# A hybrid decoder trunk: attention's opening moved ahead of the last value unit, and a second output unit moved into the early steps

## The chip, the cores and the metric

The kernel runs on one core of a Trainium2 chip. The metric is the device time of one execution in microseconds (us). A core has a matrix engine (TensorE, PE in the profile), a vector engine (VectorE, DVE), an activation engine (ScalarE, ACT), GpSimd (POOL) and SyncE (SP), which here issues the DMAs. Each engine works through its own list of instructions in order, and the lists are tied together by semaphores that the kernel sets and waits for by hand.

## The reference

Two layers over 512 tokens of width 1024. Each layer normalizes x, projects it once, and feeds the parts of the projection to four mixers (differential attention, a short gated convolution, an S5 state-space mixer with a gated output, a Mamba-2 mixer). Their outputs, 1280 channels together, go through one output projection; a gated MLP follows. The part around the change is this:

```python
for l in range(DEPTH):
    proj = rmsnorm(x, ln1_g[l]) @ w_in[l]
    ...
    # per head h of 4, per block i of 128 queries, for c in (0, 1):
    s = q[c] @ k[c].T                      # causal, scaled, q and k normalized and rotated
    p[c] = softmax(s)
    o = (p[0] - lam * p[1]) @ v            # then rmsnorm over the head's 128 channels
    ...
    g = gelu(y); o_c = g * sigmoid(g @ w_glu + b_glu)     # the S5 mixer's gate
    x = x + concat(o_a, o_b, o_c, o_d) @ w_out[l]
```

## The kernel before

**Weights come as units.** Each projection is cut into units of 128 output channels. For unit g, SP loads the weights into a raw buffer, ACT copies them to a high part `wh` (`prep`, line 1105), POOL subtracts to get the low part `wl` (`low`, line 430), and PE multiplies three times: high weights by the low and by the high part of the input, low weights by the high part. `wh` and `wl` have two buffers, used in turn. PE's `unit` (line 582) does an output or MLP unit into a bank of PSUM; `v_unit` (line 898) does one of four units of the value projection, which gather over all four into banks 0, 1, 6 and 7. These four are input units 24 to 27, the last of the input stage.

**Attention** is 16 steps, n = 0 to 15: head n // 4, query block n % 4. A step's width is 128, 256, 384 or 512 keys. Its parts are handed round the engines:

- PE `scores(n)`: the two score matrices, into banks 2 and 3 for even n, 6 and 7 for odd n.
- DVE `maxima(n)`: two row maxima. ACT `exps(n)`: two exponentials with their sums. DVE `combine(n)`: reciprocals, scaling and the difference of the two, into G.
- PE `turn(n)`: transposes that into bank 4. ACT copies it back to G (line 1363). PE `attend(n)`: multiplies by v into bank 5, one bank for each head.
- When a head is complete: DVE `head_out` copies bank 5 to `ssum`, ACT `head_square` squares it, PE `head_sum` sums it over the channels into the bank that `HEAD_BANK = [0, 0, 2, 6]` gives, ACT `head_log` and `head_rms` and DVE `head_emit` normalize.

PE runs `scores(0)` and `scores(1)` after the fourth value unit, and then in step n: `scores(n + 2)`, `turn(n)`, `attend(n - 1)`. The head sum of head 0 stands at the end of step 6, that of head 1 at the end of step 10.

**Beside the steps** PE does other work. Eight output units over the channels of mixers B and D ("early" units) can be done before attention is complete; six of them stand in the steps that `BESIDE = [1, 5, 7, 9, 13, 15]` names, between `turn` and `attend` (that of step 15 ahead of its turn), the two others behind step 15. They go into banks 0 and 1 in turn, by their place in the list. DVE's `residual` (line 1504) adds a finished one to x and frees the bank; it stands at the head of the following step. The S5 gate (`s5_glu`, two banks, 0 and 1) stands in step `GATES = 3`; ACT then loads the sigmoid's table, computes two sigmoids and loads the table of exp and ln again, DVE multiplies, and in the next step ACT and DVE split the result (`emit`, `emit_low`).

**Order on DVE.** In step n DVE does `combine(n + 1)` and `maxima(n + 2)`; the maxima come first in the steps that `MAXIMA_AHEAD = (1, 3, 4, 10, 11)` names. **Order on ACT.** In step n: `exps(n + 1)`, the copy of turn n, then the gate's part, `head_square`, a `prep` in the step after a unit, `head_log`.

**Banks are claimed.** PE waits before it writes a bank until what it held was read; `claim` notes who frees it:

```python
def claim(b, freed, k=1):
    if b in free_at:
        pe.wait_ge(*free_at[b])
    free_at[b] = (freed, raised(freed, k))
```

`unit` claims its bank with `resid` (DVE's residual frees it), and `head_sum(b)` claims bank b with `head_ln`, after it has waited for the square.

Of the kernel before, what the change touches and what calls it, by code (L numbers as in the profile page):

```python
# [11 lines left out]
ACT = mybir.ActivationFunctionType  # L12
# [3 lines left out]
D, T, P = 1024, 512, 128  # L16
KD = D // P
NQ = T // P
# [9 lines left out]
KLATE, KEARLY = MIXB, MIXED - MIXB  # L28
STEPS = HEADS * NQ
# [5 lines left out]
PAIR_STEPS, PAIR_HIGHS, PAIR_LOWS, PAIR_SUBS, PAIR_SUMS, PAIR_READS = 13, 6, 3, 4, 4, 6  # L35
PAIR_BANKS = [(6, 7, 4, 5), (2, 3, 0, 1)]
GROUPS = -(-2 * SJ // BLOCKS)
BESIDE = [1, 5, 7, 9, 13, STEPS - 1]
GATES = 3
MAXIMA_AHEAD = (1, 3, 4, 10, 11)  # L40
V_BANK = [0, 1, 6, 7]
HEAD_BANK = [0, 0, 2, 6]
WHOLE_MEAN = 5
# [36 lines left out]
def build(nc, A):  # L80
    with ExitStack() as ctx:
# [485 lines left out]
        def _(pe):  # L567
# [6 lines left out]
# [4 lines that stand above are left out]
                if freed is xbc_silu:  # L578
                    raised(unit_out)
                free_at[b] = (freed, raised(freed, k))  # L580
# [344 lines left out]
                    w = mm(bank[4][:, t:t + 1], rbc[:, t * P:(t + 1) * P], ident[:, 0:1], start=True, stop=True)  # L925
                w.then_inc(act_bank[4], 1)

            def scores(n):
                h, q = n // NQ, n % NQ
                banks = (2, 3, 6, 7)[2 * (n % 2):2 * (n % 2) + 2]  # L930
                rows = [slice(QK * c, QK * c + QK) for c in range(2)]
                qs = [qk[r, 2 * h, q * P:(q + 1) * P] for r in rows]
                last = slice(q * P, (q + 1) * P)
                for b in banks:
                    claim(b, exp_done)
                if q:
                    for c, b in enumerate(banks):
                        mm(bank[b][:, 0:q * P], qs[c], qk[rows[c], 2 * h + 1, 0:q * P], start=True, stop=True)  # L938
                for c, b in enumerate(banks):
                    mm(bank[b][:, last], qs[c], qk[rows[c], 2 * h + 1, last], start=True, stop=False)  # L940
                for b in banks:
                    mm(bank[b][:, last], cbf[:, 0, :], cbf[:, 1, :], start=False, stop=True).then_inc(dve_bank[b], 1)
# [31 lines left out]
            for l in range(L):  # L974
# [22 lines left out]
                        s5_windows(l, 0)  # L997

                for s in range(2, NIN):
                    if s >= NIN - NQ:  # L1000
                        v_unit(l, s - (NIN - NQ))
                    else:
                        unit(unit_bank(s), KD, xh, xl, xbc_silu if 2 <= s <= 7 else unit_out,
                             within=lambda: beside(s - 1))
                    if s == 2:
                        dt_turn()
                    if s == 8:
                        s5_inputs(l, 3)
                    if s == 7:
                        pe.wait_ge(xbc_silu, 6 * l + 4)  # L1010
                        m2_turn(0)
                        m2_turn(1)
                    if s == 9:
                        m2_turn(2)
                        m2_turn(3)
                        pe.wait_ge(xbc_silu, 6 * l + 6)
                        m2_states(0)
                        m2_states(1)
                    if s == 10:
                        m2_states(2)  # L1020
                        s5_kernels(l)
                    if s == 11:
                        m2_decays(1)
                        s5_windows(l, 1)
                        s5_in(l, 0)
                    if s == 12:
                        m2_apply(0)
                        m2_decays(2)
                        m2_scores(1)
                    if s == 13:  # L1030
                        m2_decays(3)
                    if s == 15:
                        m2_apply(1)
                    if s == 16:
                        m2_norm()
                    if 17 <= s <= 24:
                        qk_mean(l, s - 17)
                    if s == 25:
                        token_norm()
                    if s == 22:  # L1040
                        s5_out(l, 1)
                beside(NIN - 1)

                pe.wait_ge(qk_done, 8 * (l + 1))
                pe.wait_ge(mask_ready, 1)
                scores(0)
                scores(1)
                for n in range(STEPS):
                    if n + 2 < STEPS:
                        scores(n + 2)  # L1050
                    if n == BESIDE[-1]:
                        unit(1, KEARLY, early_hi, early_lo, resid)
                    turn(n)
                    if n == GATES:
                        s5_glu()
                    if n == BESIDE[0]:
                        pe.wait_ge(mixed_ready, nth(mixed_ready, KEARLY))
                    if n in BESIDE[:-1]:
                        unit(BESIDE.index(n) % 2, KEARLY, early_hi, early_lo, resid)
                    if n == 1:  # L1060
                        pe.wait_ge(v_ready, HEADS * (l + 1))
                    if n:
                        attend(l, n - 1)
                    if n > NQ and n % NQ == 2:
                        head_sum(HEAD_BANK[n // NQ - 1])
# [18 lines left out]
        def _(act):  # L1084
# [127 lines left out]
            for l in range(L):  # L1212
# [47 lines left out]
                def v_copy(t):  # L1260
# [3 lines left out]
                        act.wait_ge(act_bank[V_BANK[t]], nth(act_bank[V_BANK[t]]))  # L1264
                    fn(v[:, t, :], bank[V_BANK[t]][:, :], ACT.Copy, scale=token_rms[:, t:t + 1]).then_inc(v_ready, 1)

                for s in range(1, NIN):
                    prep()
                    if 6 <= s <= 10:
# [55 lines left out]
                    if s == 26:  # L1325
                        gelu(0)
                        gelu(1)
                        ln_exp_tables()

                def exps(n):  # L1330
                    w, s = (n % NQ + 1) * P, n % 2
                    for c in range(2):
                        act.wait_ge(exp_go, nth(exp_go))
                        fn(G[:, 2 * s + c, 0:w], bank[(2, 3, 6, 7)[2 * s + c]][:, 0:w], ACT.Exp,  # L1334
                           bias=soft[:, s, c:c + 1], accum_out=soft[:, s, 2 + c:3 + c]).then_inc(exp_done, 1)

                def head_square():
                    act.wait_ge(head_copied, nth(head_copied))
# [11 lines left out]
                act.wait_ge(token_ready, l + 1)  # L1350
                v_copy(2)
                v_copy(3)
                exps(0)
                v_copy(0)
                v_copy(1)
                for n in range(STEPS):
# [84 lines left out]
        def _(dve):  # L1441
# [554 lines left out]
            for l in range(L):  # L1996
# [4 lines left out]
                for s in range(2, NIN):  # L2001
# [86 lines left out]
                    if s in (21, 25):  # L2088
                        s5_finish(l, (s - 21) // 4)
                maxima(0)  # L2090
                maxima(1)
                combine(l, 0)
                for n in range(STEPS):
                    if n - 1 in BESIDE:
                        residual(BESIDE.index(n - 1), BESIDE.index(n - 1) % 2)
                    if n in MAXIMA_AHEAD:
                        maxima(n + 2)
# [1 line left out]
                        combine(l, n + 1)  # L2099
                    if n + 2 < STEPS and n not in MAXIMA_AHEAD:  # L2100
                        maxima(n + 2)
                    if n == GATES:
                        for i, (gate, gated) in enumerate(((sA, sC), (sB, sD))):
                            dve.wait_ge(glu_full, nth(glu_full))
                            tt(gated[:, :].rearrange("p (c t) -> p t c", t=CH),
                               *[k.rearrange("p (t c) -> p t c", t=CH) for k in (gate[:, :], u[:, i, :])],
                               MUL).then_inc(em_full, 1)
# [167 lines left out]
```

## Time and profile before

| what | value |
|---|---|
| median of 3 runs | 1295.24 us |
| range of the runs | 1295.24 to 1295.95 us |
| the profiled execution | 1294.14 us |
| its span, first to last instruction | 1292.4 us |
| PE busy | 1282.8 us (99%) |
| DVE busy | 996.9 us (77%) |
| POOL busy | 636.7 us (49%) |
| ACT busy | 533.6 us (41%) |

The profile is of one execution. Its time is 1.7 us longer than its span, and 1.1 us shorter than the median of the runs. The timeline view, of which most rows below are, lists instructions by start; neighbours of one kind are merged into a row with their count. The ends of PE's matmuls are modelled and overlap the start of the next, so the distance from start to start is what an instruction takes of PE's time. Attention lies at about 206 to 258 us in layer 0 and at about 844 to 896 us in layer 1.

### The profile page before, as it was taken

The numbers are of one execution on the slowest core, as the hardware profiler recorded it, in microseconds if no ns is written. First come the engines' busy times: TensorE is split into PE (matmuls) and PEld (weight loads), VectorE is DVE, ScalarE is ACT, GpSimd is POOL, SyncE is SP. The second block draws the span as 40 slices with busy tenths as digits, with TensorE's granted clock in tenths as the row PEclk, the third lists the DMA queues.
The fourth block names the chain that finished last, engine by engine and source line by source line (L and its number), as shares of the span: only waits on it lengthen the run. The fifth ranks groups of instructions, "written<-read, shape, count | busy, mean of one in ns | idle before, by whom it ended". The sixth has DMA issues, their size and how long they took to land.

```text
span 1292.4 us, 17677 instructions
## 1 busy us (share of the span) xinstructions
PE 1282.8 (99%) x6790; PEld 1075.5 (83%) x6790; DVE 996.9 (77%) x1376; ACT 533.6 (41%) x836; POOL 636.7 (49%) x314
## 2 busy tenths in 40 slices
PE   9999999999999999999999999999999999999999
PEld 6888887788888998888878888877888889888898
DVE  8789895846899868876237798777478998689997
ACT  6332556644333422233334235476442333323342
POOL 2986661244445344444458775612444443444532
PEclk9999999999999999999999999999999999999999
DMA  6232321033333233333233213211333333232323
GB/s 225 82 99 66 91 88 42 26 97 114 98 86 128 91 91 96 98 98 112 84 99 98 82 54 112 80 30 53 99 102 95 97 101 120 91 96 87 125 96 103
DMA packets 40947, 120.59 MB, mean 93 GB/s; under 512 B 6432, under 2 KB 10656, under 8 KB 40864
## 3 DMA queue, kind: packets, MB, share of 16 engines
q1 hardware_dynamic: 40864, 119.46, 29.8%
q8 instruction: 54, 0.88, 0.3%
q14 instruction: 29, 0.24, 0.1%
HBM read 114.20 MB, written 2.10 MB: 90 GB/s over the span
## 4 chain that ended last, share of the span: by engine, by line
PE 91%; DVE 4%; POOL 2%; ACT 2%; DMA 1%; issue 0%; SPq 0%; POOLq 0%
PE bank L599 22%; PE bank L612 22%; PE bank L604 21%; PE bank L650 12%; PE bank L911 3%; PE bank L959 1%; POOL wl L430 1%; DMA raw<-in_w_in 1%; PE bank L601 1%; PE bank L938 1%; PE bank L948 1%; PE bank L856 1%; ACT G L1334 1%; PE bank L789 1%; PE bank L804 1%; PE bank L813 1%
## 5 line engine op out<-in xcount | busy, mean ns | idle before, releaser
L430 POOL TENSOR_TENSOR wl<-raw,wh 128x1024 fp32r<-128x1024 f32 (+3 forms) x184 | 441.5, 2401 | 512.9 <-ACT wh L1105 423.5
L599 PE MATMUL bank<-xl,wh 128*128 128x512 f32 x1088 | 279.8, 395 | 0.7 <-DVE xl L1461 0.7
L612 PE MATMUL bank<-xh,wl 128*128 128x512 f32 x1088 | 272.4, 392 | 0.0
L604 PE MATMUL bank<-xh,wh 128*128 128x512 f32 x1056 | 261.0, 389 | 0.0
L1105 ACT ACTIVATE wh<-raw 128x1024 fp32r<-128x1024 f32 (+3 forms) x184 | 185.8, 1010 | 144.7 <-PE bank L604 81.2
L599 PEld LDWEIGHTS bank<-xl,wh 128*128 128x128 f32 x1088 | 202.4, 188 | 48.2 <-issue 4.3
L612 PEld LDWEIGHTS bank<-xh,wl 128*128 128x128 f32 x1088 | 203.2, 188 | 43.0 <-issue 1.4
L604 PEld LDWEIGHTS bank<-xh,wh 128*128 128x128 f32 x1056 | 198.2, 188 | 41.6
L447 POOL TENSOR_TENSOR wl<-raw,wh 128x768 fp32r<-128x768 f32 (+1 forms) x36 | 65.2, 1813 | 99.4 <-ACT wh L1109 67.8
L1406 ACT ACTIVATE G<-G 128x512 f32<-128x512 f32 x44 | 27.8, 633 | 181.4 <-DVE G L1487 181.4
L1109 ACT ACTIVATE wh<-raw 128x640 fp32r<-128x640 f32 (+2 forms) x72 | 60.4, 862 | 91.9 <-DVE raw L1922 32.7
L1504 DVE TENSOR_TENSOR x<-x,bank 128x512 f32<-128x512 f32 x40 | 27.4, 685 | 80.2 <-PE bank L612 80.0
L1475 DVE TENSOR_TENSOR G<-bank,rbc 128x512 f32<-128x512 f32 x68 | 46.5, 684 | 34.1 <-PE bank L612 34.1
L1475 DVE TENSOR_TENSOR pad<-bank,rbc 128x512 f32<-128x512 f32 x60 | 41.2, 687 | 39.5 <-PE bank L612 28.6
L599 PE MATMUL bank<-ml,wh 128*128 128x512 f32 x248 | 68.9, 401 | 0.0
L1487 DVE SCALAR_TENSOR_TENSOR G<-pad,par_all,G 128x512 f32<-128x512 f32 x48 | 66.5, 1385 | 1.7
L1482 DVE TENSOR_SCALAR G<-pad,par_all 128x512 f32<-128x512 f32 x48 | 65.5, 1365 | 1.6
L612 PE MATMUL bank<-mh,wl 128*128 128x512 f32 x248 | 63.3, 389 | 0.0
L1907 DVE TENSOR_TENSOR x<-x,bank 128x256 f32<-128x256 f32 (+1 forms) x72 | 41.7, 593 | 21.5 <-PE bank L667 16.3
L604 PE MATMUL bank<-mh,wh 128*128 128x512 f32 x225 | 57.2, 390 | 0.0
L1889 DVE TENSOR_TENSOR wl<-raw,wh 128x640 fp32r<-128x640 f32 x48 | 53.3, 1130 | 4.4 <-ACT wh L1109 4.3
L1167 ACT ACTIVATE xh<-x,par_all 128x512 fp32r<-128x512 f32 x32 | 23.1, 721 | 79.6 <-DVE x L1504 77.6
(345 smaller groups left out, 2097.2 us busy)
## 6 DMA issues: line engine op xcount, KB each, us to landing
raw<-in_w_gu SPq DMA_DIRECT2D x88, 512.0 KB, 3.6
raw<-in_w_in SPq DMA_DIRECT2D x52, 512.0 KB, 3.8
raw<-in_w_dn SPq DMA_DIRECT2D x32, 704.0 KB, 4.1
raw<-in_w_ol SPq DMA_DIRECT2D x16, 384.0 KB, 3.1
raw<-in_w_oe SPq DMA_DIRECT2D x16, 256.0 KB, 2.6
x<-in_x SPq DMA_DIRECT2D x8, 256.0 KB, 5.8
raw<-in_w_first SPq DMA_DIRECT2D x4, 512.0 KB, 4.1
out_x<-x SPq DMA_DIRECT2D x8, 256.0 KB, 4.8
```

What stands on the lines that cost most here:

```text
L430: tt(wl[:, p, 0:cols], raws[RAW[g][0]][:, 0:cols], wh[:, p, 0:cols].bitcast(F32), ALU.subtract).then_inc(wl_full, 1)
L447: tt(wl[:, p, cols], raws[PAIR_RAW[load][0]][:, cols], wh[:, p, cols].bitcast(F32), ALU.subtract).then_inc(pair_low, 1)
L599: mm(bank[b][:, :], wh[:, p, k * P:(k + 1) * P], lo[:, k, :], start=(k == 0), stop=False)
L604: w = mm(bank[b][:, :], wh[:, p, k * P:(k + 1) * P], hi[:, k, :], start=False, stop=False)
L612: w = mm(bank[b][:, :], wl[:, p, k * P:(k + 1) * P], hi[:, k, :], start=False, stop=(k == K - 1))
L650: i = mm(out, w[:, at[0], at[1] + k * P:at[1] + (k + 1) * P], b, start=start and k == 0, stop=stop and k == KW - 1, skip_group_check=True)
L1105: fn(wh[:, p, 0:cols], raws[r][:, 0:cols], ACT.Copy).then_inc(wh_full, 1)
L1109: fn(wh[:, p, to], raws[PAIR_RAW[2 * j + p][0]][:, of], ACT.Copy).then_inc(pair_high, 1)
L1475: tt(out, bank[b][:, :].rearrange(order, **sizes), rbc[:, :].rearrange(order, **sizes), MUL).then_inc(unit_out, 1)
L1482: after(ts(out, pad[:, p, 4:4 + T], weights[n - 1], None, MUL))
L1487: return stt(out, pad[:, p, 5 - n:5 - n + T], weights[0], out, MUL, ADD)
L1889: tt(wl[:, p, to], of, wh[:, p, to].bitcast(F32), SUB).then_inc(pair_sub, 1)
```

## The change

`scores(0)`, `maxima(0)`, `exps(0)` and `combine(0)` move ahead. PE does `scores(0)` before the fourth value unit, ACT does `exps(0)` before the `prep` of the loop's last step, and DVE does `combine(0)` before `maxima(1)`. After the last value unit PE does `scores(2)` and then `scores(1)`. The unit of step 7 moves to step 2, and the units of steps 1 and 2 (`UNIT_AHEAD`) stand ahead of the step's scores instead of behind its turn. The gate moves from step 3 to step 4. On DVE the maxima come first in other steps, and in steps 2, 3, 6 and 14 (`ADD_LATE`) the residual stands behind `combine` and `maxima`. The wait before a score bank is written is now spelled out by the step's number, since the steps' scores are no longer issued in order. `HEAD_BANK` and `unit` are as before.

```diff
-BESIDE = [1, 5, 7, 9, 13, STEPS - 1]
-GATES = 3
-MAXIMA_AHEAD = (1, 3, 4, 10, 11)
+BESIDE = [1, 2, 5, 9, 13, STEPS - 1]
+GATES = 4
+MAXIMA_AHEAD = (0, 1, 5, 6, 7, 11)
+UNIT_AHEAD = (1, 2)
+ADD_LATE = (2, 3, 6, 14)
...
-            def scores(n):
+            def scores(l, n):
...
-                for b in banks:
-                    claim(b, exp_done)
+                for c, b in enumerate(banks):
+                    if b in free_at:
+                        pe.wait_ge(*free_at[b])
+                    free_at[b] = (exp_done, 2 * (STEPS * l + n) + c + 1)
...
                 for s in range(2, NIN):
+                    if s == NIN - 1:
+                        pe.wait_ge(qk_done, 8 * (l + 1))
+                        pe.wait_ge(mask_ready, 1)
+                        scores(l, 0)
                     if s >= NIN - NQ:
                         v_unit(l, s - (NIN - NQ))
...
-                pe.wait_ge(qk_done, 8 * (l + 1))
-                pe.wait_ge(mask_ready, 1)
-                scores(0)
-                scores(1)
+                def early_unit(n):
+                    if n == BESIDE[0]:
+                        pe.wait_ge(mixed_ready, nth(mixed_ready, KEARLY))
+                    unit(BESIDE.index(n) % 2, KEARLY, early_hi, early_lo, resid)
+
+                scores(l, 2)
+                scores(l, 1)
                 for n in range(STEPS):
-                    if n + 2 < STEPS:
-                        scores(n + 2)
+                    if n in UNIT_AHEAD:
+                        early_unit(n)
+                    if 0 < n < STEPS - 2:
+                        scores(l, n + 2)
                     if n == BESIDE[-1]:
-                        unit(1, KEARLY, early_hi, early_lo, resid)
+                        early_unit(n)
                     turn(n)
                     if n == GATES:
                         s5_glu()
-                    if n == BESIDE[0]:
-                        pe.wait_ge(mixed_ready, nth(mixed_ready, KEARLY))
-                    if n in BESIDE[:-1]:
-                        unit(BESIDE.index(n) % 2, KEARLY, early_hi, early_lo, resid)
+                    if n in BESIDE[:-1] and n not in UNIT_AHEAD:
+                        early_unit(n)
...
                         gelu(0)
                         gelu(1)
                         ln_exp_tables()
+                        exps(0)
...
                 v_copy(2)
                 v_copy(3)
-                exps(0)
                 v_copy(0)
                 v_copy(1)
...
                 maxima(0)
+                combine(l, 0)
                 maxima(1)
-                combine(l, 0)
                 for n in range(STEPS):
-                    if n - 1 in BESIDE:
+                    if n - 1 in BESIDE and n not in ADD_LATE:
                         residual(BESIDE.index(n - 1), BESIDE.index(n - 1) % 2)
                     if n in MAXIMA_AHEAD:
                         maxima(n + 2)
...
                     if n + 2 < STEPS and n not in MAXIMA_AHEAD:
                         maxima(n + 2)
+                    if n - 1 in BESIDE and n in ADD_LATE:
+                        residual(BESIDE.index(n - 1), BESIDE.index(n - 1) % 2)
```

## Rows read from the trace of the kernel before

**Rows 1.** The page: busy us of each engine, share of the span, instructions.

```profile
PE 1282.8 (99%) x6790; PEld 1075.5 (83%) x6790; DVE 996.9 (77%) x1376; ACT 533.6 (41%) x836; POOL 636.7 (49%) x314
```

**Rows 2.** The waits of PE: total us, times, longest.

```profile
PE bank L938 <- ACT G L1334: 2.7, 6, 0.5
```

**Rows 3.** Timeline of PE, opening of attention in layer 0: start, duration, line.

```profile
202.02 1.98 PE L911 MATMUL bank<-wh,xh 128*128 128x512 f32 x8
203.84 1.98 PE L911 MATMUL bank<-wl,xh 128*128 128x512 f32 x8
205.74 0.49 PE L940 MATMUL bank<-qk 64*128 64x128 f32 x4
...
207.03 0.28 PE L942 MATMUL bank<-cbf 128*128 128x128 bf16 x2
207.71 0.70 PE L938 MATMUL bank<-qk 64*128 64x256 f32 x4 [0.40 <-ACT G L1334]
...
208.57 0.28 PE L942 MATMUL bank<-cbf 128*128 128x128 bf16 x2
...
209.78 0.92 PE L938 MATMUL bank<-qk 64*128 64x384 f32 x4 [0.50 <-ACT G L1334]
```

**Rows 4.** Timeline of ACT and DVE in the same stretch.

```profile
204.09 0.63 ACT L1105 ACTIVATE wh<-raw 128x512 fp32r<-128x512 f32 x1 [1.04 <-PE bank L911]
204.63 1.25 ACT L1265 ACTIVATE v<-bank,token_rms 128x512 f32<-128x512 f32 x2
...
206.43 0.49 DVE L1833 TENSOR_REDUCE soft<-bank 128x1 f32<-128x128 f32 x2 [9.34 <-PE bank L942]
```

**Rows 5.** Timeline of PE, steps 4 to 10 of layer 0.

```profile
221.93 0.29 PE L942 MATMUL bank<-cbf 128*128 128x128 bf16 x2
222.05 0.28 PE L948 MATMUL bank<-cst,G 128*128 128x128 f32 x1
222.17 1.06 PE L959 MATMUL bank<-G,v 128*128 128x128 f32 x8
223.68 0.92 PE L938 MATMUL bank<-qk 64*128 64x384 f32 x4 [0.45 <-ACT G L1334]
...
231.11 0.28 PE L942 MATMUL bank<-cbf 128*128 128x128 bf16 x2
231.46 0.66 PE L948 MATMUL bank<-cst,G 128*128 128x128 f32 x4
...
236.56 1.06 PE L959 MATMUL bank<-G,v 128*128 128x128 f32 x8
...
243.34 1.02 PE L967 MATMUL bank<-pad,cst 128*128 128x512 f32 x2
```

**Rows 6.** Timeline, all engines, from the gate's end to step 7.

```profile
220.31 0.83 PE L959 MATMUL bank<-G,v 128*128 128x128 f32 x6
...
220.51 0.69 ACT L1367 ACTIVATE s5b<-bank,par_all 128x512 f32<-128x512 f32 x1 [0.73 <-PE bank L813]
...
222.51 0.47 ACT L1334 ACTIVATE G<-bank,soft 128x256 f32<-128x256 f32 x1
...
223.58 0.64 ACT L1195 ACTIVATE mh<-s5c 128x512 fp32r<-128x512 f32 x1
...
224.62 0.59 ACT L1334 ACTIVATE G<-bank,soft 128x384 f32<-128x384 f32 x1
...
225.74 0.40 ACT L1363 ACTIVATE G<-bank 128x256 f32<-128x256 f32 x1
...
228.38 0.69 ACT L1334 ACTIVATE G<-bank,soft 128x512 f32<-128x512 f32 x1 [1.21 <-DVE soft L1833]
...
228.86 0.68 DVE L1504 TENSOR_TENSOR x<-x,bank 128x512 f32<-128x512 f32 x1
...
229.86 0.17 DVE L1840 RECIPROCAL soft<-soft 128x2 f32<-128x2 f32 x1 [0.32 <-ACT G L1334]
...
231.31 0.48 DVE L1833 TENSOR_REDUCE soft<-bank 128x1 f32<-128x128 f32 x2
```

More of the change, by code:

```diff
@@ L1265, in v_copy, with exps @@
                     fn(v[:, t, :], bank[V_BANK[t]][:, :], ACT.Copy, scale=token_rms[:, t:t + 1]).then_inc(v_ready, 1)
+                def exps(n):
+                    w, s = (n % NQ + 1) * P, n % 2
+                    for c in range(2):
+                        act.wait_ge(exp_go, nth(exp_go))
+                        fn(G[:, 2 * s + c, 0:w], bank[(2, 3, 6, 7)[2 * s + c]][:, 0:w], ACT.Exp,
+                           bias=soft[:, s, c:c + 1], accum_out=soft[:, s, 2 + c:3 + c]).then_inc(exp_done, 1)
                 for s in range(1, NIN):
@@ L1328, in _ @@
                         ln_exp_tables()
[L1330 to L1335, printed above, removed]
+                        exps(0)
                 def head_square():
```

## The prediction, made before the changed kernel was run

> **What bounds the kernel now.** I read the page first. PE is busy for 1282.8 us, 99% of the span [rows 1], so PE's list sets the end, and no PE instruction is added or removed. The change can give only what PE waits for inside attention, and can cost only new waits there. Second, the waits of PE: it waited 6 times for the exponentials before it could write a score bank [rows 2], which is three times in each layer. This view's 2.7 us is low, since modelled ends cover part of each wait. So I went, third, to PE's timeline and measured from start to start.
>
> Two prices come from a place without a wait. The two mask matmuls (L942) take 222.05 − 221.93 = 0.12 us, and a turn of one block takes 222.17 − 222.05 = 0.12 us [rows 5]. An `attend` of four blocks is eight such matmuls of 128 columns, 8 × 0.122 = 0.98 us, so the scores of step 5 could have begun at 222.17 + 0.98 = 223.15.
>
> Against these prices PE loses, in layer 0:
>
> - before `scores(2)`: 207.71 − 207.03 − 0.12 = 0.56 us [rows 3];
> - around `turn(0)` and before `scores(3)`: 209.78 − 208.57 − 2 × 0.12 = 0.97 us [rows 3] (`turn(0)` waits for `combine(0)`, then the scores for `exps(1)`);
> - before `scores(7)`: 223.68 − 223.15 = 0.53 us [rows 5]. `exps(5)` stands behind the sigmoids and two table loads;
> - before `turn(7)`: 231.46 − 231.11 − 0.12 = 0.23 us [rows 5].
>
> Together 2.29 us. Layer 1 shows the same waits, so 4.58 us is the most that these four can give. That is 0.35% of the time. About 0.2%, or 2.6 us, is what a measurement of this kernel can tell from no change.
>
> **The change part by part.**
>
> *The opening, −1.53 us a layer.* `scores(0)` now stands before the fourth value unit, whose three passes of 203.84 − 202.02 = 1.82 us [rows 3] run from 200.2 to 205.65. DVE has been idle for 9.34 us when `maxima(0)` comes at 206.43 [rows 4], so it takes the maxima at once, near 201.4. ACT is idle for 1.04 us before 204.09 [rows 4]. `exps(0)` starts in that hole, at 203.05, and takes less than 223.58 − 222.51 = 1.07 us, which holds a wider pair and a copy [rows 6]; so it delays nothing by more than 0.03. `combine(0)` follows on an idle DVE and takes less than the widest one's 1.45 (below): done before 205.6. `turn(0)` needs it only after 207, so that wait goes. `scores(2)` finds its banks free, so the 0.56 goes. The value unit runs 0.6 to 0.7 us later and pulls `prep` and the value copies with it: the two that `scores(1)` needs end near 205.88 + 0.7 = 206.6 [rows 4], and `scores(1)` comes near 207.4 because `scores(2)` is ahead of it. That is hidden by 0.8 us. `scores(3)` needs `exps(1)`: `scores(1)` ends near 208.2, its maxima take half a microsecond, and the exponentials at most the 1.07, so near 209.8; ahead of it PE now has the unit of step 1 (2.8 us), so it comes near 211.2. The 0.97 goes as well. Of the unit of step 2 the same holds: behind it stand `scores(4)`, `turn(2)` and `attend(1)`, whose inputs come some 0.5 us or more before they are needed. Without the unit as cover, `scores(4)` would wait as `scores(3)` did, up to 0.97 us.
>
> *Splitting the value units, +0.15 us a layer.* PE goes over from value to score matmuls twice instead of once. Before, that step costs 205.74 − (203.84 + 1.82) = 0.08 us [rows 3]. The way back is shown nowhere. I take 0.15 in all: below, nothing, if the weight loads overlap; above, 0.32, four such steps.
>
> *The gate a step later, −0.53 us a layer.* `exps(5)` now stands before the sigmoids, so `scores(7)` finds it done. `scores(8)` needs `exps(6)`, which ends about 3.4 us after the gate's matmuls (0.20 + 2.00 + 1.12, below). PE gets there only after about 5.4 us, with the unit of step 5 between. The gate's second bank was last used by the unit of step 2. Its residual ends near 220.7 and the matmuls for that bank begin near 222.0, so it is hidden by 1.3 us.
>
> *DVE's new order, −0.23 us a layer.* `combine(7)` is done before PE comes to `turn(7)`, because of the next term.
>
> *A new wait at the head sum, +2.07 us a layer.* The unit of step 5 was second in the list of units and used bank 1. Now it is third and uses bank 0. The head sum of head 0 stands in step 6 and claims bank 0. So PE cannot begin it before `residual` has freed the bank, and in step 6 this residual is one of those put behind `combine(7)`, which needs `exps(7)`. I count from the end of the gate's last matmul, E (220.31 in rows 6).
>
> ACT and DVE: the second sigmoid starts at E + 0.20. It and a table load take 222.51 − 220.51 = 2.00. `exps(6)` is 384 wide: 225.74 − 224.62 = 1.12. The copy of turn 5 is 256 wide: 0.40, of which 0.10 overlaps, so 0.30. Two `emit` and the `head_square` take 0.52 each, by (224.62 − 223.58) / 2: together 1.56. `exps(7)` to the reciprocal is 229.86 − 228.38 = 1.48. `combine(7)` is 231.31 − 229.86 = 1.45. The residual is 0.68, and 0.06 more until PE sees it [all rows 6]. The sum is 0.20 + 2.00 + 1.12 + 0.30 + 1.56 + 1.48 + 1.45 + 0.68 + 0.06 = 8.85 us.
>
> PE in the same time: `attend(3)`, `scores(7)`, `turn(5)`, the unit, `attend(4)`, `scores(8)`, `turn(6)`, `attend(5)`. Steps 7 to 10 of before hold the same pieces in the same widths and order, from `attend(7)` to the head sum of head 1, without a wait: 243.34 − 236.56 = 6.78 us [rows 5].
>
> PE is at the head sum 8.85 − 6.78 = 2.07 us too early. Bounds: 1.7 if ACT's instructions overlap by 0.04 us more each; 2.5 if DVE is last instead. DVE's own list (gate products, `head_out`, `maxima(7)`, `combine(6)`, two `emit_low`, `maxima(8)`) comes out only 0.1 us ahead of ACT. Queued behind the waiting head sum is all of PE. ACT's `head_log` waits for the sum, and `exps(8)` stands behind it. Step 7 has no unit any more. By the same prices `scores(10)` and `turn(8)` still find their inputs some 0.2 us early.
>
> The Trainium skill speaks against this sum at one place. "ScalarE: Activation LUTs", section "What ACT_TABLE_LOAD costs", gives every change of table about 1.38 us of drain beside its load of 1.28 us. Rows 6 show 2.00 us for sigmoid (0.69) and load together, so there is no room for a drain and I use the row. By the page the stall would be 1.38 us longer.
>
> *Prep, POOL and the DMAs.* The third and fourth weights of this stage are prepared in steps 2 and 3 instead of 2 and 6, each ahead of its use by several us. SP's and POOL's lists keep their order; I price this at nothing, since the unit that uses the fourth comes only in step 9. If ACT's extra 0.5 us in step 3 were not covered, `exps(5)` would be that much later, and it has 4 us.
>
> Sum for a layer: −1.53 + 0.15 − 0.53 − 0.23 + 2.07 = −0.07 us. For two layers it is −0.14 us, on the profiled execution's 1294.14 us; the median of the runs is 1.1 us above that, so I forecast 1295.24 − 0.14 = 1295.1 us.
>
> **The rivals.**
>
> *The head sum does not wait.* If bank 0 is free in time (the residual early, or ACT's chain 2 us shorter than I make it), the gain stays: 2 × (−2.14) = −4.3 us, 1291.0 us. For it speaks that my chain has nine terms. Against it: every one is read from a row, and all nine would have to be half a term wrong in one direction.
>
> *The opening gives half.* If `turn(0)` or `scores(3)` still waits (value copies late behind `prep`), 0.75 us a layer is lost: 1296.6 us. The margins of 0.5 to 0.8 us speak against it.
>
> *Steps 8 to 10 come apart (slower).* After the late head sum, `head_log`, `exps(8)`, `head_rms` and the copy of turn 7 run one behind the other on ACT with no unit on PE as cover. If they are over 0.2 us slower than I make them, `scores(10)`, `turn(8)` and `scores(11)` wait as the narrow steps of the opening did. The price is that of the waits of before at the same kinds of place, 0.56 + 0.97 + 0.53 = 2.06 us a layer: 1295.1 + 4.1 = 1299.2 us. It decides from the 0.2 us on. Against it: these parts are short and read from rows of the same widths.
>
> *A drain at the tables (slower).* If something follows the second table load that rows 6 do not show, the head sum waits longer by it. It would take 1.3 us a layer to matter: 1295.1 + 2.6 = 1297.7 us. The page's 1.38 us would make it 1297.9 us. Rows 6 speak against it.
>
> **How the numbers follow.** The forecast has 0.70, the half opening 0.08, the head sum without a wait 0.12, steps 8 to 10 apart 0.08, the drain 0.02. The forecast's own range: the terms' bounds give a layer −2.29 + 0 + 1.7 = −0.59 to −2.29 + 0.32 + 2.5 = +0.53 us, so −1.2 to +1.1 us about 1295.24; the runs differ by 0.7 us, mostly upward: 1293.6 to 1297.0 us. To hold 8 in 10 it must reach into the others on both sides, to 1292.5 and 1297.5 us. Faster by over 0.2% (below 1292.6): the first rival and a tail of the forecast, 0.14. Slower by over 0.2% (above 1297.8): the last two, 0.10. Within: 0.76.
>
> **What the profile of after would show.** Right: in each layer no PE wait before `scores(2)`, `turn(0)`, `scores(3)` and `scores(7)`; `scores(0)` before the last three passes of L911; a gap of about 2 us before the first head sum (L967), which ends on DVE's residual (L1504); that residual behind the 512-wide `combine(7)`. Attention then begins earlier and ends where it ended. Wrong: a first head sum without a gap makes it 1291; gaps at L938 and L948 in steps 8 to 11 make it slower.

## The result, and the profile after

The changed kernel takes 1297.04 us, the kernel before 1295.15 us (medians of 21 runs each, in turn on the same chip). The ratio is 1.0015, with a 95% interval of 1.0009 to 1.0021. The forecast was 1295.1 us, so the change costs 1.9 us where I had it at nothing. 1297.04 lies inside the stated range of 1292.5 to 1297.5, and just outside the 1293.6 to 1297.0 that the forecast's own terms gave. Times, medians and ratios here leave out one disturbed run, one of the twelve of e7_gate3, which took 1419.12 us at a mean clock of 0.849.

The waits of PE in the changed kernel (total, times, longest) hold the forecast's new wait, and the six waits of [rows 2] are gone:

```profile
PE bank L971 <- DVE x L1515: 3.9, 2, 2.0
```

L971 is the head sum's matmul and L1515 the residual (L967 and L1504 before). Next, the timeline of PE: the opening and the steps to 7 in layer 0.

```profile
199.34 1.97 PE L913 MATMUL bank<-wl,xh 128*128 128x512 f32 x8
201.24 0.49 PE L944 MATMUL bank<-qk 64*128 64x128 f32 x4
...
205.50 1.98 PE L913 MATMUL bank<-wl,xh 128*128 128x512 f32 x8
207.41 0.70 PE L942 MATMUL bank<-qk 64*128 64x256 f32 x4
...
209.25 0.28 PE L952 MATMUL bank<-cst,G 128*128 128x128 f32 x1
209.29 1.17 PE L601 MATMUL bank<-ml,wh 128*128 128x512 f32 x4
...
212.20 0.92 PE L942 MATMUL bank<-qk 64*128 64x384 f32 x4
...
224.61 1.05 PE L963 MATMUL bank<-G,v 128*128 128x128 f32 x8
225.59 0.92 PE L942 MATMUL bank<-qk 64*128 64x384 f32 x4
...
230.96 0.61 PE L963 MATMUL bank<-G,v 128*128 128x128 f32 x4
233.52 1.30 PE L971 MATMUL bank<-pad,cst 128*128 128x512 f32 x2 [1.95 <-DVE x L1515]
234.75 0.80 PE L942 MATMUL bank<-qk 64*128 64x128 f32 x4
...
236.09 1.06 PE L952 MATMUL bank<-cst,G 128*128 128x128 f32 x4
236.95 1.19 PE L963 MATMUL bank<-G,v 128*128 128x128 f32 x6
238.07 0.70 PE L942 MATMUL bank<-qk 64*128 64x256 f32 x4
```

`scores(0)` stands at 201.24 inside the value units. After them, `scores(2)`, `turn(0)` (209.25), `scores(3)` (212.20) and `scores(7)` (225.59) follow on what is ahead of them without a wait, where [rows 3] and [rows 5] have gaps. PE comes to the head sum at 230.96 + 0.45 = 231.41 (an `attend` of four matmuls and 0.45 us, as at 229.06 and 229.51 before) and starts it at 233.52. The timeline of DVE shows what it waits for, the end of `combine(7)` and behind it the residual:

```profile
232.02 0.75 DVE L1853 SCALAR_TENSOR_TENSOR G<-G,soft 128x512 f32<-128x512 f32 x1
232.69 0.68 DVE L1515 TENSOR_TENSOR x<-x,bank 128x512 f32<-128x512 f32 x1
```

The rows behind the head sum are the news: the same matmuls take nearly twice as long as before the wait. The turn of four blocks takes 236.95 − 236.09 = 0.86 us, in layer 1 (below) 0.44. The windows view of the changed kernel shows why (the columns after the stretch: PE, PEld, DVE, ACT and POOL busy, the granted clock, DMA share, GB/s):

```profile
225.00:231.00 6.00, 6.00 (x42) 4.76 (x42) 5.67 (x12) 5.97 (x14) 0.00 (x0) 1.00 0.00 0
233.50:238.00 4.50, 4.48 (x22) 3.27 (x22) 1.70 (x6) 2.71 (x8) 0.40 (x1) 0.62 0.20 62
873.40:876.40 3.00, 2.96 (x22) 2.03 (x22) 0.99 (x4) 1.83 (x7) 0.42 (x1) 1.00 0.32 90
```

After the wait TensorE's granted clock is at the lower of its two levels, 1.2 instead of 2.4 GHz, for most of 233.5 to 238. In this execution that happened in layer 0 only. In layer 1 the clock stayed, and the timeline of PE shows the same wait and then the usual durations:

```profile
873.44 1.10 PE L971 MATMUL bank<-pad,cst 128*128 128x512 f32 x2 [1.95 <-DVE x L1515]
874.46 0.49 PE L942 MATMUL bank<-qk 64*128 64x128 f32 x4
...
875.23 0.60 PE L952 MATMUL bank<-cst,G 128*128 128x128 f32 x4
875.67 0.83 PE L963 MATMUL bank<-G,v 128*128 128x128 f32 x6
876.44 0.70 PE L942 MATMUL bank<-qk 64*128 64x256 f32 x4
```

From the head sum to `scores(10)` it is 238.07 − 233.52 = 4.55 us in layer 0 and 876.44 − 873.44 = 3.00 us in layer 1. The difference, 1.55 us, is the price of one fall. The runs agree. 18 of the changed kernel's 21 runs have a mean clock below 1.000. Their spans are 1294.9 to 1295.8 us where it is 0.999 (12 runs) and 1296.1 to 1297.8 us at 0.997 and less (6 runs). The three at 1.000 have 1292.8, 1293.4 and 1293.8 us; the kernel before has a median span of 1293.4 to 1293.6 us in its runs beside the experiments. So without the falls the change gives nothing, as the sum said, and with them it costs 1.9 us. An estimate: if 0.999 stands for one fall and the lower clocks for two, as in p1 and p2 below, there are 24 falls in 21 runs, and 24 / 21 × 1.55 = 1.8 us.

### The profile page after: what moved, and what is told of

Same layout as the page of the kernel before. It is cut to its first block, busy times and chain, and to the rows that moved or that the text cites. A ratio compares the mean times of both kernels' runs of the same rounds, so it can differ in the third digit from the quotient of the medians.

```text
span 1295.2 us, 17677 instructions
## 1 busy us (share of the span) xinstructions
PE 1283.8 (99%) x6790; PEld 1075.1 (83%) x6790; DVE 996.5 (77%) x1376; ACT 533.9 (41%) x836; POOL 636.5 (49%) x314
## 4 chain that ended last, share of the span: by engine, by line
PE 92%; DVE 4%; POOL 2%; DMA 1%; ACT 1%; issue 0%; SPq 0%; POOLq 0%
PE bank L601 22%; PE bank L614 22%; PE bank L606 21%; PE bank L652 12%; PE bank L913 3%; PE bank L963 1%; PE bank L942 1%; POOL wl L432 1%; DMA raw<-in_w_in 1%; PE bank L603 1%; PE bank L952 1%; PE bank L858 1%; PE bank L944 1%; PE bank L971 1%; PE bank L791 1%; PE bank L806 1%
## 5 line engine op out<-in xcount | busy, mean ns | idle before, releaser
L1515 DVE TENSOR_TENSOR x<-x,bank 128x512 f32<-128x512 f32 x40 | 27.4, 684 | 79.8 <-PE bank L614 79.7
```

## The experiments

**The head sum's wait taken away (e1_bank1).** Head 0's sum goes to bank 1, which nobody uses in step 6.

```diff
-HEAD_BANK = [0, 0, 2, 6]
+HEAD_BANK = [1, 0, 2, 6]
```

> The changed kernel with the first head sum in bank 1 instead of bank 0, so that it does not wait for the residual of the unit of step 5. Theory 1 (the wait of 2.0 to 2.1 us at the head sum costs its own length in each layer, and in some executions TensorE's granted clock falls to 1.2 GHz behind it, which costs some 1.6 us more each time): no wait at the first head sum, mean clock 1.000 in every run, 1297.0 - 2 x 2.1 - 1.9 = 1290.9 us, 0.3% below before, and runs close together. Theory 2 (the clock and the spread of the runs have nothing to do with this wait): the wait goes but the clock stays at 0.999 and below in most runs: about 1292.8 us, still spread over 5 us.

Measured: 1290.95 us (1290.75 to 1291.36), ratio 0.9967 (0.9955 to 0.9980), all five runs with clock 1.000 and spans of 1289.0 to 1289.6 us. The timeline of PE at the head sum:

```profile
230.68 0.61 PE L963 MATMUL bank<-G,v 128*128 128x128 f32 x4
231.13 1.02 PE L971 MATMUL bank<-pad,cst 128*128 128x512 f32 x2
```

The sum starts 0.45 us after the start of `attend(5)`, as without a wait. This constant decides the change: with it, a gain of 4.3 us; without, a loss of 1.9 us.

**The residual of step 6 early again (e2_resid_first).**

```diff
-ADD_LATE = (2, 3, 6, 14)
+ADD_LATE = (2, 3, 14)
```

> The changed kernel with the residual of step 6 at the head of the step again; the head sum stays in bank 0. Theory 1: DVE does the residual as soon as the unit is done, about 0.7 us after it and before the head sum comes, so the wait is gone or under 0.3 us: 1290.9 to 1291.5 us, clock 1.000. combine(7) comes 0.6 us later, which turn(7) does not feel. Theory 2: about 1292.8 us with a clock below 1. If not the residual but something else holds bank 0, the wait stays and the time is 1297.

Measured: 1293.04 us (1292.33 to 1296.51), ratio 0.9985 (0.9976 to 0.9994), ten of eleven runs at clock 1.000. The wait at the head sum went, but one that I had ruled out came. The timeline of PE:

```profile
231.24 1.10 PE L971 MATMUL bank<-pad,cst 128*128 128x512 f32 x2
...
232.91 0.28 PE L946 MATMUL bank<-cbf 128*128 128x128 bf16 x2
233.87 0.66 PE L952 MATMUL bank<-cst,G 128*128 128x128 f32 x4 [0.67 <-DVE G L1853]
```

`turn(7)` starts 0.96 us after the mask matmuls instead of 0.12: it waits for `combine(7)`. The residual pushes that back by 0.43 us only (its last instruction starts at 232.18, in e1_bank1 at 231.75). The larger part is that this instruction takes 1.64 us here and 0.75 in e1_bank1. The timelines of DVE and POOL in e2_resid_first, and behind the dots those of e1_bank1:

```profile
232.18 1.64 DVE L1853 SCALAR_TENSOR_TENSOR G<-G,soft 128x512 f32<-128x512 f32 x1
231.97 1.30 POOL L432 TENSOR_TENSOR wl<-raw,wh 128x512 fp32r<-128x512 f32 x1 [10.26 <-ACT wh L1116]
...
231.75 0.75 DVE L1853 SCALAR_TENSOR_TENSOR G<-G,soft 128x512 f32<-128x512 f32 x1
231.97 1.67 POOL L432 TENSOR_TENSOR wl<-raw,wh 128x512 fp32r<-128x512 f32 x1 [10.26 <-ACT wh L1116]
```

Here it begins 0.21 us after POOL's `low` and is the slow one of the two; in e1_bank1 it begins 0.22 us before, and POOL's is. Layer 1 has the same 1.64 us. Without it `combine(7)` would have been done just in time for `turn(7)`. That POOL's instruction is the reason is read from rows, here and in the last section, and was not tested.

**TensorE kept busy through the wait (e3_fill, e8_fill4).** Matmuls into the free bank 1, with a result that is used nowhere, ahead of the head sum of step 6, nine of them in the first kernel (below) and four in the second.

```diff
                     if n > NQ and n % NQ == 2:
+                        if n == NQ + 2:
+                            pe.wait_ge(*free_at[1])
+                            for _ in range(9):
+                                mm(bank[1][:, :], wh[:, 1, 0:P], early_hi[:, 0, :], start=True, stop=True)
                         head_sum(HEAD_BANK[n // NQ - 1])
```

> The changed kernel with nine matmuls of 128x512 (9 x 0.23 = 2.05 us) into bank 1, which is free there, ahead of the first head sum: their result is used nowhere. The head sum still starts when the residual is done, but TensorE is not idle before it. Theory 1: clock 1.000 in every run, 1295.0 to 1295.3 us, as before. Theory 2 (what costs the extra 1.9 us is not the idle time): 1297.0 us as in the changed kernel, with clocks below 1.

> As the kernel with nine matmuls ahead of the first head sum, but with four (0.9 us), so that TensorE is idle for some 1.1 us there instead of 2.0 or none. Taken by spans, since the kernel with nine lay 2.5 us under its time and not 1.8. Theory 1 (idle time at the head sum lets the granted clock fall, the more often the longer it is): clock below 1.000 in fewer runs than the 18 of 21 of the changed kernel and in more than the 3 of 11 with nine matmuls; median span between 1294.3 and 1295.2 us. Theory 2 (the number of falls has nothing to do with idle time): as often as in the changed kernel, 1295.2 us.

Measured with nine: 1296.57 us (1295.39 to 1298.64), ratio 1.0011 (1.0002 to 1.0020). Its time lies further above its span than in the other kernels (2.0 us in the median and up to 2.75, elsewhere 1.8), so spans are the better measure: the median is 1294.3 us, against 1295.2 in the changed kernel and 1293.5 in the kernel before beside it. The clock is 1.000 in 8 of 11 runs. Theory 1 had said all, and the time of before; of the 0.8 us that are missing, some 0.4 remain in the runs at 1.000 (median span 1293.9 against 1293.5 us), and I did not trace them. With four: 1295.61 us, ratio 1.0005 (0.9996 to 1.0014), median span 1293.8 us, idle 1.0 us at each head sum, clock 1.000 in 9 of 11 runs. Both theories missed here: theory 1 wanted more falls than with nine matmuls and a span of 1294.3 us or more. The timeline of PE with nine matmuls, and the window around it:

```profile
231.07 2.31 PE L1079 MATMUL bank<-mh,wh 128*128 128x512 f32 x9
233.28 1.10 PE L971 MATMUL bank<-pad,cst 128*128 128x512 f32 x2
```

```profile
231.00:236.00 5.00, 5.00 (x33) 3.54 (x33) 2.84 (x8) 2.51 (x8) 1.68 (x1) 1.00 0.19 52
```

The head sum starts as late as in the changed kernel, so the wait is all there. Only the idle time is gone, and with it most of the falls (3 of 11 runs instead of 18 of 21). So it is the idle time that brings the fall, not the late start. Going from nine matmuls to four, from no idle time to 1.0 us, adds no falls that these runs can show (3 and 2 of 11). The remaining ones contradict theory 1 as I had put it, with 1.000 in every run; p4 below shows one place where they can come from.

**The same wait in the kernel before (e4_before_wait).** Head sum in bank 1, which the unit of step 5 uses there, and the residual of step 6 behind `combine` and `maxima`.

```diff
-HEAD_BANK = [0, 0, 2, 6]
+HEAD_BANK = [1, 0, 2, 6]
...
-                    if n - 1 in BESIDE:
+                    if n - 1 in BESIDE and n != 6:
...
+                    if n - 1 in BESIDE and n == 6:
+                        residual(BESIDE.index(n - 1), BESIDE.index(n - 1) % 2)
```

> The kernel before with the same wait built in and nothing else of the change: first head sum in bank 1, which the unit of step 5 uses there, and the residual of step 6 behind combine(7) and maxima(8). From the rows of before the head sum would start at 232.45 instead of 229.51, 2.9 us late, of which 0.2 us replaces the wait before turn(7). Theory 1: a wait of 2.9 us in each layer with a fall of the clock behind it in most runs: 1295.2 + 5.4 + 1.6 to 3.2 = 1302 to 1304 us, clock 0.996 to 0.999. Theory 2: 1300.6 us, clock 1.000.

Measured: 1304.63 us (1303.33 to 1305.93), ratio 1.0071 (1.0059 to 1.0084), all five runs at 0.996 or 0.997. The waits of PE, and windows behind the two head sums:

```profile
PE bank L967 <- DVE x L1504: 5.8, 2, 2.9
```

```profile
233.00:238.00 5.00, 4.63 (x20) 2.98 (x21) 1.66 (x6) 2.53 (x8) 0.35 (x1) 0.66 0.18 56
...
876.00:881.00 5.00, 5.00 (x19) 3.08 (x20) 1.59 (x6) 2.64 (x8) 0.00 (x0) 0.50 0.19 52
```

The wait is 2.9 us as worked out, and 4.0 us more is lost: the clock falls behind both. In layer 1 the fall lasts about twice as long as the others that the traces show (the granted clock is 0.50 from about 875.5 to 882.3 us, elsewhere for 3 to 4 us). So wait and fall need nothing of the change but the bank and the residual's place.

**One wait instead of two (e9_wait_l0).**

```diff
+HEAD_BANK = [1, 0, 2, 6]
...
+                        head_sum(0 if l == 0 and n == 6 else HEAD_BANK[n // NQ - 1])
```

(and the same bank for ACT's `head_log`)

> The changed kernel with the first head sum in bank 0 in layer 0 only and in bank 1 in layer 1: one wait of 2.0 us instead of two. Theory 1: 1290.95 + 2.1 = 1293.1 us where the clock holds, and up to 1.7 us more in the runs in which it falls, so a median of 1293.1 to 1294.8, clocks of 1.000 and 0.999 and never below 0.998. Theory 2: 1293.1 us.

Measured: 1294.59 us (1292.85 to 1297.68), ratio 0.9996 (0.9987 to 1.0005). By the mean clock of the execution: four runs at 1.000 with spans of 1291.1 to 1291.6, four at 0.998 with 1292.6 to 1293.5, three at 0.996 or 0.997 with 1295.0 to 1295.9 us. At clock 1.000 the three kernels with two, one and no wait have median spans of 1293.4, 1291.3 and 1289.1 us, so each wait costs 2.1 to 2.2 us by itself. The three low runs contradict my expectation of at most one fall of 1.7 us.

**Where the falls stand (p1 to p4).** Profiles again: twice the changed kernel, twice the kernel with one wait.

> The changed kernel unchanged, for a second profile. Its first one fell in clock in layer 0 only. Theory 1: waits of 2.0 us at both first head sums again, and any stretch with a granted clock below 1.00 begins within a few us of one of them; which layers fall differs from execution to execution. Theory 2: a fall stands somewhere else in the span.

> The changed kernel unchanged, for a third profile: theory 1 as in the second (each fall within a few us of a wait at a first head sum), theory 2 a fall elsewhere.

> The kernel with the wait in layer 0 only, again: 3 of its 11 runs had a clock of 0.996 to 0.997 and spans 4 us above the fastest, more than one fall of 1.7 us. Theory 1a: the fall behind the one wait can last about twice as long, in one piece. Theory 1b: a second fall stands somewhere else, without a wait of this kind ahead of it. With a clock of 0.998 or 1.000 in this profile it stays open.

> The kernel with the wait in layer 0 only, a third profile: theory 1a one longer fall behind the wait if the clock is 0.997 or less, theory 1b a second fall somewhere else.

Measured (one execution each, beside 1294.37 us for the kernel before): p1 1296.55 us, clock 0.999, with a fall in layer 0 only; p2 1297.88 us, 0.997, with falls in both layers; p3 1292.99 us, 1.000, with none; p4 1296.04 us, 0.997, with a fall behind its one wait and another elsewhere. Windows of p2 behind the head sums of the two layers:

```profile
233.00:239.00 6.00, 5.71 (x34) 4.36 (x35) 3.17 (x10) 3.42 (x11) 0.68 (x1) 0.72 0.18 46
872.00:877.00 5.00, 4.02 (x19) 2.32 (x20) 1.39 (x4) 1.94 (x7) 1.36 (x1) 0.66 0.20 54
```

The windows of p4, and its waits:

```profile
10.00:15.00 5.00, 4.60 (x9) 2.06 (x9) 4.68 (x6) 3.82 (x8) 2.11 (x1) 0.66 1.04 406
235.00:241.00 6.00, 5.96 (x36) 4.69 (x37) 3.03 (x9) 3.53 (x12) 0.41 (x1) 0.72 0.18 46
```

```profile
PE bank L601 <- ACT wh L1116: 2.2, 1, 2.2
PE bank L971 <- DVE x L1515: 2.0, 1, 2.0
```

The second fall of p4 stands at the kernel's start. There TensorE had waited 2.2 us for the first weights, and in that execution longer than in the others (1.2 us at most in the other profiles). So this low run has a second fall, as theory 1b says, but again behind a wait of about 2 us. Theory 1a is not excluded for the low runs of e9_wait_l0, which have no profile: layer 1 of e4_before_wait has one fall of twice the usual length. The start is the same in every kernel here and can explain falls where the head sum is filled or does not wait; for those runs it was not looked at.

**The opening alone (e5_open_only).** The changed kernel with the constants of before and no unit ahead.

```diff
-BESIDE = [1, 2, 5, 9, 13, STEPS - 1]
-GATES = 4
-MAXIMA_AHEAD = (0, 1, 5, 6, 7, 11)
-UNIT_AHEAD = (1, 2)
-ADD_LATE = (2, 3, 6, 14)
+BESIDE = [1, 5, 7, 9, 13, STEPS - 1]
+GATES = 3
+MAXIMA_AHEAD = (1, 3, 4, 10, 11)
+UNIT_AHEAD = ()
+ADD_LATE = ()
```

> The opening alone: scores, maxima, exponentials and combination of step 0 ahead of the last value unit, with the units, the gate and DVE's order as before. By rows of before the waits ahead of scores(2) and turn(0) go (0.82 us a layer), but scores(3) now comes right behind turn(0), at about 208.4, and needs exps(1), done at 209.8: it starts near 209.95, where it started at 209.78 before. So the opening without a unit as cover gives nothing: theory 1: 1295.2 + 2 x 0.17 = 1295.6 us, and up to 3 us more where the clock falls behind the new wait of 1.5 us. Theory 2 (the opening gives its own share whatever stands ahead of scores(3)): 1295.2 - 2 x 0.7 = 1293.8 us.

Measured: 1295.42 us (1294.87 to 1297.52), ratio 1.0004 (0.9995 to 1.0013). The timeline of PE:

```profile
208.88 0.28 PE L952 MATMUL bank<-cst,G 128*128 128x128 f32 x1
210.65 0.92 PE L942 MATMUL bank<-qk 64*128 64x384 f32 x4 [1.49 <-ACT G L1282]
```

The kernel before is at 1295.14 us beside it. All the time won at `scores(2)` and `turn(0)` is lost again ahead of `scores(3)`. The early step 0 is worth something only with a unit ahead of `scores(3)`.

**The fast variant without the opening (e6_no_open).** `scores(0)` and `exps(0)` where they were, `combine(0)` behind `maxima(1)`, the rest as in e1_bank1.

```diff
-                    if s == NIN - 1:
...
-                        scores(l, 0)
...
+                scores(l, 0)
+                scores(l, 1)
                 scores(l, 2)
-                scores(l, 1)
...
```

(and the same on ACT, with `exps(0)` between the value copies, and on DVE)

> The fast variant (first head sum in bank 1) without the opening: scores(0), scores(1) and scores(2) after the last value unit, exps(0) behind the value copies as before; units, gate and DVE's order as changed. The waits ahead of scores(2) and turn(0) come back, 0.82 us a layer, and the split of the value units goes, 0.15: theory 1: 1290.95 + 2 x 0.67 = 1292.3 us. Theory 2 (most of the opening's gain comes from the early step 0, not from the unit ahead of scores(3)): 1290.95 + 2 x 1.4 = 1293.8 us.

Measured: 1292.87 us (1291.96 to 1294.34), ratio 0.9982 (0.9973 to 0.9991); at clock 1.000 a median span of 1290.8 us against 1289.1. The opening is worth 1.7 us with a unit as cover, 0.85 a layer, or 1.9 us by the median times. The timeline of PE, the first pass of the fourth value unit and `scores(3)`:

```profile
200.60 1.98 PE L913 MATMUL bank<-wh,xl 128*128 128x512 f32 x8
...
212.36 0.92 PE L942 MATMUL bank<-qk 64*128 64x384 f32 x4
```

That is 11.76 us, and in the changed kernel, from where the third value unit is done, 212.20 − 201.15 = 11.05: 0.71 us less, in layer 1 0.72. The two waits make 0.82, so splitting the value units costs 0.1 us. The rest of what the runs show, 0.1 to 0.3 us a layer, I did not trace.

**The fast variant with the gate in step 3 (e7_gate3).**

```diff
-GATES = 4
+GATES = 3
```

> The fast variant (first head sum in bank 1) with the gate in step 3 as before. exps(5) stands behind the sigmoids and two table loads again; with the units of steps 1 and 2 ahead nothing else covers it, so scores(7) waits by rows of before 0.53 us, less what one unit fewer behind it leaves: theory 1: 1290.95 + 2 x 0.53 = 1292.0 us. Theory 2 (the later gate gives nothing of its own): 1291.0 us.

Measured: 1297.88 us (1296.99 to 1301.38), ratio 1.0022 (1.0013 to 1.0031), some 7 us above e1_bank1 where I had expected 1. The waits of PE:

```profile
PE bank L952 <- DVE G L1853: 2.1, 2, 1.1
PE bank L942 <- ACT G L1282: 1.9, 2, 1.0
PE bank L815 <- DVE x L1515: 1.4, 2, 0.7
```

The gate now waits for the late residual of the unit of step 2, whose bank it needs. That pushes back its sigmoids, `exps(5)` and `combine(6)`, and each of them keeps PE waiting. So the gate's move is no gain of 0.5 us beside the others: with this order on DVE it is what makes the units of steps 1 and 2 possible. Whether an early residual in step 3 would do as well was not run.

**A last wait in the fast variant (e10_tuned).**

```diff
-MAXIMA_AHEAD = (0, 1, 5, 6, 7, 11)
-ADD_LATE = (2, 3, 6, 14)
+MAXIMA_AHEAD = (0, 1, 5, 6, 7, 9, 11)
+ADD_LATE = (2, 3, 6, 10, 14)
```

> The fast variant (first head sum in bank 1) with maxima(11) ahead of combine(10) in step 9 and the residual of step 10 put late, so that combine(11) is done before turn(11), which waits some 0.2 to 0.3 us in each layer in the fast variant: 1290.95 - 2 x 0.2 = 1290.5 us if exps(11) follows its maxima at once, 1291.0 us if ACT's own list holds it.

Measured: 1290.99 us (1290.14 to 1292.33), ratio 0.9967 (0.9955 to 0.9979), the same as e1_bank1. The timeline of PE:

```profile
241.35 0.29 PE L946 MATMUL bank<-cbf 128*128 128x128 bf16 x2
241.72 0.55 PE L952 MATMUL bank<-cst,G 128*128 128x128 f32 x3
...
244.15 0.28 PE L946 MATMUL bank<-cbf 128*128 128x128 bf16 x2
244.28 0.61 PE L952 MATMUL bank<-cst,G 128*128 128x128 f32 x4
```

The wait before `turn(11)` is gone (0.13 us apart), but `turn(10)` has one of 241.72 − 241.35 − 0.12 = 0.25 us: `maxima(11)` now stands ahead of `combine(10)`. The wait moved by a step. The time is the second of the two expected, but not for the reason given there, that ACT's own list holds `exps(11)`: `combine(11)` was done in time.

## Why the prediction was wrong

*The opening.* Right. `exps(0)` ran at 204.0 in ACT's hole, and no wait was left before `scores(2)`, `turn(0)` and `scores(3)`. From the fourth value unit's turn to the end of the gate, before took 220.31 − 200.2 = 20.1 us; after took 224.61 − 201.15 = 23.5 us and did 4.7 us more work in it (`scores(6)`, `turn(4)`, `attend(2)`, one unit). That is a gain of 1.3 us; forecast was 1.53 − 0.15. The two waits, 0.56 and 0.97 us, are one chain: e5_open_only shows that the early step 0 without a unit behind it gives nothing, e6_no_open that with the unit it is worth about what its own two waits cost. The 0.15 us for splitting the value units measured 0.1.

*The gate and `turn(7)`.* Right for the wait before `scores(7)`, which is gone in the changed kernel. The 0.53 us is not the gate's own, as e7_gate3 shows. The 0.23 us at `turn(7)` is right in size, but not for the reason given, that PE comes late: in e1_bank1, where the head sum does not wait, `turn(7)` starts 232.85 − 232.73 = 0.12 us after the mask matmuls too. DVE's new order gives it alone. Layer 1 lost a further 0.14 us at `turn(11)`, for which the sum has no term.

*The new wait at the head sum.* Right in place, releaser and size. From the end of the gate, 224.61, to the head sum it is 233.52 − 224.61 = 8.91 us (forecast 8.85), and PE was there after 231.41 − 224.61 = 6.80 us (6.78). The wait is 2.11 us, forecast 2.07. e1_bank1 came out at 1290.95 us, where the first rival had put a kernel without this wait, 1291.0 us.

*The sum.* At full clock it holds. Three such runs of the changed kernel have spans of 1292.8 to 1293.8 us around the 1293.4 to 1293.6 of before, for a forecast of −0.14 us.

*The step that failed* is the price of the wait at the head sum. I charged "8.85 − 6.78 = 2.07 us" and nothing for what an idle TensorE does to its own clock afterwards. The bounds, 1.7 and 2.5 us, were bounds of the wait's length only. What the runs showed in its place: a wait of 2.0 us costs 2.1 us by its length and, behind somewhat more than half of such waits, another 1.55 us by a granted clock at its lower level for some 3 to 4 us. (The 24 falls estimated above would be 24 of 42 waits; in the profiles it is five of nine.) e4_before_wait reproduces it in the kernel before, e3_fill removes most of it with the head sum as late as ever. The kernel before gave no row for this: its longest wait inside attention is 0.5 us by the profile [rows 2], with a clock of 1.00 throughout, and I did not ask what a wait four times as long would do. That 1297.04 us lies inside the stated range is luck: the range was drawn wider than the sum's to hold the rivals, and none of them is what came. The Trainium skill has the rule, in "TensorE: Matmul & The Clock Gate", section "Part 1: The HAM clock gate (the "warmup" mystery)": the array's full clock is granted for activity, and idle time takes it away. The traces agree in kind: the granted clock was 1.00 before the wait and 0.62 in the stretch behind it.

*The table drain* did not come: in the timeline of ACT in the changed kernel the exponentials start 226.81 − 225.51 = 1.30 us after the start of the table load, which itself takes 1.28, and the chain's 8.91 us leaves no room for a drain.

```profile
225.51 1.28 ACT L1196 ACT_TABLE_LOAD   x1
226.81 0.58 ACT L1282 ACTIVATE G<-bank,soft 128x384 f32<-128x384 f32 x1
```

*Steps 8 to 10* did not come apart either: PE's list of waits shows nothing there.

## What to carry to other kernels

When a list of bank numbers goes by position, moving one entry changes the parity of all behind it: look up who else claims the bank that a moved unit now lands in. Price a new wait of the matrix engine twice, its length and what the granted clock does behind it, and ask of each new wait whether it is longer than any in the profile at hand. A wait that is taken from one place gives its time only if the next instruction that could wait is covered too (the early step 0 needed a unit, the units needed the gate moved), so such edits are to be summed as a chain and not one by one.

## What the runs showed of the hardware

Waits of TensorE of 2.0 us and more bring falls of its granted clock, and not in each execution of one kernel. With 2.9 us in both layers all 5 runs had a mean clock below 1.000, with 2.0 us in both layers 18 of 21, with 2.0 us in one layer 7 of 11. With shorter waits the counts do not differ from those of the kernel before: 3 of 11 with 1.5 us in both layers (e5_open_only), 2 of 11 with 1.0 us, 3 of 11 with the wait filled, 1 of 11 in e2_resid_first, 1 of 11 in e7_gate3, 2 of 11 in e6_no_open, none of 5 in e1_bank1, 1 of 5 in e10_tuned, and 11 of the 71 runs of the kernel before beside e1 to e10. Falls at the start, behind a wait for the first weights as in p4, are in these counts.

The sixteen profiles say the same place by place. Both head sums with a wait of 2.9 us have a fall around them, and five of the nine with 2.0 us; the two waits of 1.5 us and the two of 1.0 us have none. Elsewhere the granted clock is below 1.00 only at the start of p4 and in the last few us of most executions. A fall does not always begin with the wait's end: in the changed kernel it came 0.8 us after the head sum's start, in p2 0.1 us before it in layer 1 and 1.3 us after it in layer 0. What decides between two executions with the same wait stays open: p1 and p2 are one kernel with the same two waits, one with a fall in layer 0 only and one with a fall in both.

A 512-wide DVE instruction with two tensors of SBUF as input, begun while POOL's `low` is at work, ended 0.53 to 0.56 us after POOL's, in all 26 cases found around attention in the nine profiles that were read for this (before, after, and e1, e2, e4 to e7, e10). It took 1.64 us instead of 0.75 in e2_resid_first (both layers), and in the kernel before 1.34 instead of 0.68 at 238.10 and 1.10 instead of 0.74 at 256.62. The residual, which reads a bank, took its usual 0.68 us beside a `low` in e1_bank1 (232.42). No run tested this by itself.
